# PEER V experts 0 to 119 with standing weights and moving tokens; fetched V rows scaled on ScalarE and summed on Pool

## What is computed

```python
def step(args):
    xc, ic, gc = args
    u = expert_u[ic]
    hval = jnp.einsum('cd,chkd->chk', xc, u).astype(jnp.float32)
    a = (gc * jax.nn.gelu(hval, approximate=False)).astype(xc.dtype)
    return jnp.einsum('chk,chkd->cd', a, expert_v[ic])
...
h = h + peer_ffn(rms_norm_2(h, norm_ffn_g[l]), ...)
return rms_norm_2(h, norm_final_g)
```

## Time and profile before

| | before |
|---|---|
| median of 3 runs | 1364.8 us (1364.66 to 1365.86) |
| the profiled execution | 1366.88 us |
| its span, first to last instruction | 1365.1 us |
| TensorE busy | 1349.6 us, 99% |
| VectorE busy | 1060.6 us, 78% |
| ScalarE busy | 818.7 us, 60% |
| Pool busy | 161.5 us, 12% |
| DMA, mean over the span | 202 GB/s |

### The profile page before, as it was taken

The page is one execution under the profiler, slowest core; times in us unless marked ns, Lnnn a source line. Parts: engine busy times, 40 slices in busy tenths (PEclk is TensorE's granted clock), DMA queues, the critical chain, the costliest instruction groups (busy, mean ns, idle before and its releaser), DMA issues.

```text
span 1365.1 us, 21297 instructions
## 1 busy us (share of the span) xinstructions
PE 1349.6 (99%) x7896; PEld 1169.7 (86%) x7896; DVE 1060.6 (78%) x1965; ACT 818.7 (60%) x1568; POOL 161.5 (12%) x128
## 2 busy tenths in 40 slices
PE   8999999999999999999999999999999999999998
PEld 6998888888898888789999999999877777777776
DVE  6878676666787567679999899998887777777775
ACT  6876555555665554555556988886554444544444
POOL 3002030000000000000001100001333332333200
PEclk9999999999999999999999999999999999999999
DMA  6533466566544446655655544445889877777763
GB/s 223 185 120 116 136 221 187 189 194 189 167 159 137 141 139 228 203 169 172 214 188 189 193 157 153 157 156 184 298 285 348 291 286 267 280 291 287 274 197 100
DMA packets 77372, 275.38 MB, mean 202 GB/s; under 512 B 9845, under 2 KB 10357, under 8 KB 76886
## 3 DMA queue, kind: packets, MB, share of 16 engines
q1 hardware_dynamic: 67462, 239.52, 53.0%
q0 software_dynamic: 9808, 34.51, 6.6%
HBM read 270.94 MB, written 2.10 MB: 200 GB/s over the span
## 4 chain that ended last, share of the span: by engine, by line
PE 91%; DVE 4%; ACT 2%; issue 1%; DMA 1%; POOL 0%; SPq 0%; POOLq 0%; ACTq 0%; DVEq 0%
PE bank L2335 89%; DVE wl L624 1%; PE bank L2433 1%; DMA raw<-in_wts 1%; PE bank L2421 1%; ACT wh L1688 1%; DVE rows L1562 0%; ACT kdz L1694 0%; DVE St L814 0%; DVE x L1123 0%; DVE sgt L1121 0%; DVE t L774 0%; DVE us L1553 0%; DVE sg L768 0%; DVE St L811 0%
## 5 line engine op out<-in xcount | busy, mean ns | idle before, releaser
L624 DVE TENSOR_TENSOR wl<-raw,wh 128x1024 fp32r<-128x1024 f32 x429 | 523.0, 1226 | 178.3 <-ACT wh L1688 174.0
L1688 ACT ACTIVATE wh<-raw 128x1024 fp32r<-128x1024 f32 x429 | 449.1, 1055 | 240.8 <-PE bank L2335 232.4
L2335 PE MATMUL bank<-hTb,wh 128*128 128x224 f32 (+4 forms) x2208 | 560.8, 332 | 1.8 <-DVE wl L624 1.8
L2335 PE MATMUL bank<-wh,hTb 128*128 128x512 f32 (+1 forms) x1496 | 431.1, 395 | 2.2 <-DVE hTb L658 1.5
L2335 PE MATMUL bank<-hTb,wl 128*128 128x224 f32 (+2 forms) x1640 | 426.7, 274 | 0.0
L2335 PEld LDWEIGHTS bank<-hTb,wh 128*128 128x128 f32 (+1 forms) x2208 | 372.2, 190 | 26.7 <-ACT ga L2217 1.8
L2335 PEld LDWEIGHTS bank<-wh,hTb 128*128 128x128 f32 (+1 forms) x1496 | 267.5, 180 | 78.3 <-DVE hTb L1605 2.5
L2335 PEld LDWEIGHTS bank<-hTb,wl 128*128 128x128 f32 (+1 forms) x1640 | 312.1, 190 | 6.1
L2335 PE MATMUL bank<-wl,hTb 128*128 128x512 f32 (+1 forms) x748 | 247.6, 392 | 0.0
L2335 PEld LDWEIGHTS bank<-wl,hTb 128*128 128x128 f32 (+1 forms) x748 | 134.4, 180 | 36.2
L601 POOL DMA_INDIRECT rows<-in_u_rows,expert x32 | 55.9, 1745 | 299.0 <-DVE dots L1562 295.3
(11 more groups left out here) (410 smaller groups left out, 1382.9 us busy)
## 6 DMA issues: line engine op xcount, KB each, us to landing
raw<-in_wts SPq DMA_DIRECT2D x441, 512.0 KB, 3.5
x<-in_x SPq DMA_DIRECT2D x4, 256.0 KB, 7.4
sk<-in_sk SPq DMA_DIRECT2D x1, 1024.0 KB, 7.1
spill<-x SPq DMA_DIRECT2D x1, 1024.0 KB, 7.4
x<-spill SPq DMA_DIRECT2D x1, 1024.0 KB, 6.4
gb<-in_g_ffn SPq DMA_DIRECT2D x1, 512.0 KB
gb<-in_norm_mix_g SPq DMA_DIRECT2D x1, 512.0 KB
gb<-in_norm_ffn_g SPq DMA_DIRECT2D x1, 512.0 KB, 4.2
```

What stands on the lines that cost most here:

```text
L624: e.tensor_tensor(b[:, :], raw[u % RAW][:, :], a[:, :].bitcast(F), ALU.subtract).then_inc(S("lo"), 1)
L1688: e.activation(parts_of(u)[0][:, :], raw[u % RAW][:, :], ACT.Copy).then_inc(S("hi"), 1)
L2335: return e.matmul(o, l, r, start=first, stop=last, skip_group_check=True)
```

## The change

**V units 0 to 119** (`DENSE` = 120) are computed like U units: `part_V` holds a slice of 128 output columns of V in the array, and moves 448 token columns with `wh` and 224 with `wl`. Slice k sums up in its own bank (`BANK_OF`), so that all eight banks are in use and hold the result transposed: 128 output columns by tokens. V units 120 to 127 stay as they were. Around the stage:

- U units 126 and 127 are finished inside the U loop. V units 0 and 1 first do the slices of banks 0, 1, 6, 7, and the others after the last U sum.
- V units 116 to 119 (`HOLD` = 4) are held together: first the slices in banks 0 to 3 for all four, then those in banks 4 to 7. ScalarE copies the low halves of the banks out (`lows_out`) and VectorE adds the others (`evacuated`), into places of `gates` that are no longer needed. After V unit 121 TensorE turns the eight sums back (16 transposes, into banks 4 to 7), and VectorE adds them into x (`add_turned`).
- The V rows: ScalarE multiplies the fetched row by its factor (`row_scaled`), in the row's own buffer, every 2.25 units from V unit 44 on; Pool adds it to `acc` (`added`). VectorE keeps the dots and the folding.
- `high_of` and `low_of` now stand ahead of `high` and `low` in each pass. The semaphore `one` is renamed `ready`.

```diff
+HOLD = 4
+DENSE = NE - 8
...
+        BANK_OF = (0, 1, 6, 7, 2, 3, 4, 5)
+        FIRST, SECOND = (0, 1, 4, 5), (2, 3, 6, 7)
...
+            def added(j):
+
+                e.wait_ge(S("ready"), 1 + j - SLOTS)
+                e.wait_ge(S("used"), used_by(j - 1))
+                e.tensor_tensor(acc[:, :], acc[:, :], rows[j % 3][:, :], ALU.add).then_inc(S("used"), 1)
+
             for j in range(2 * SLOTS):
+                if j >= SLOTS + 3:
+                    added(j - 2)
                 if j >= 3:
                     e.wait_ge(S("used"), used_by(j - 3))
...
+            for j in range(2 * SLOTS - 2, 2 * SLOTS):
+                added(j)
...
-                e.wait_ge(S("used"), used_by(j - 1))
-                e.scalar_tensor_tensor(out=acc[:, :], in0=t[:, :], scalar=factor[:, k:k + 1], in1=acc[:, :], op0=ALU.mult,
-                                       op1=ALU.add).then_inc(S("used"), 1)
...
+            def evacuated(ks, n):
+
+                for k in ks:
+                    e.wait_ge(S("u_out"), nth_sum("U", NE + n))
+                    e.tensor_tensor(sums_of(k), B[BANK_OF[k]][:, 0:TN], sums_of(k), ALU.add).then_inc(S("u_sum"), 1)
+                    n += 1
...
             for n in range(NE):
-                low(nth("D", "peer_expert_v_2", ORDER[n]) + LOOK)
                 if n + 2 < NE:
                     low_of(n + 2)
-                if n in (1, 2):
-                    summed(NE - 3 + n)
-                    gated(NE - 3 + n)
-                if n in at_v:
+                if n == DENSE - HOLD + 1:
+                    evacuated(FIRST, 0)
+                low(nth("D", "peer_expert_v_2", ORDER[n]) + LOOK)
+                if at_v.get(n, SLOTS + 1) <= SLOTS:
                     slot_taken(at_v[n])
-                elif n - 6 in (max(at_v), max(at_v) + 1, max(at_v) + 2):
-                    folded(n - 6 - max(at_v))
+                elif n in (DENSE - 3, DENSE - 2, DENSE - 1):
+                    folded(n - DENSE + 3)
+                if n == DENSE:
+                    evacuated(SECOND, 4)
+                elif n in (DENSE + 3, DENSE + 4):
+                    add_turned(n - DENSE - 3)
...
+                    e.activation(t[:, :], t[:, :], ACT.Copy, scale=factor[:, k:k + 1]).then_inc(S("ready"), 1)
+
+            rows_at = {after_dots + 3 + 9 * k // 4: SLOTS + k for k in range(SLOTS)}
...
+            def part_V(held, n, ks):
+
+                both = both_of(n)
+                for k in ks:
+                    c, b = two(128, k), B[BANK_OF[k]]
+                    mm(b[:, 0:2 * TN], held[0][:, c], both, n == 0, False)
+                    t = mm(b[:, 0:TN], held[1][:, c], both[:, 0, :], False, n == DENSE - 1)
+                return t
...
+            for n in range(2, DENSE - HOLD):
+                part_V(expert_of(n), n, range(8)).then_inc(S("done"), 1)
+            held = []
+            for n in range(DENSE - HOLD, DENSE):
+                held.append(expert_of(n))
+                t = part_V(held[-1], n, FIRST)
+            t.then_inc(S("half"), 1)
+            for n in range(DENSE - HOLD, DENSE):
+                part_V(held[n - DENSE + HOLD], n, SECOND).then_inc(S("done"), 1)
+            e.wait_ge(S("u_sum"), nth_sum("U", NE + 3))
```

More of the change, by code:

```diff
@@ L129, in program @@
         X0 = at[0]
-        ah = [sb(f"ah{i}", [128, 256], FR) for i in range(2)]
-        al = [sb(f"al{i}", [128, 256], FR) for i in range(2)]
+        ab = [sb(f"ab{i}", [128, 2, 256], FR) for i in range(2)]
+        ah, al = [t[:, 0, :] for t in ab], [t[:, 1, :] for t in ab]
         ge = [sb(f"ge{i}", [128, 256]) for i in range(2)]
@@ L659, in turn_low @@
                                 ALU.subtract).then_inc(S("hT_lo"), 1)
-            e.memset(one1[:, :], 1.0).then_inc(S("one"), 1)
+            e.memset(one1[:, :], 1.0).then_inc(S("ready"), 1)
             half_sums(0, 0)
@@ L1607, in vector @@
             at_u, at_v = slots_taken()
-            for n in range(GATED, NE - 2):
-                summed(n)
-                low(nth("U", ORDER[n]) + 2)
+            for n in range(GATED, NE):
+                if n < NE - 1:
+                    summed(n)
+                    low(nth("U", ORDER[n]) + 2)
+                else:
+                    low(nth("U", ORDER[n]) + 2)
+                    summed(n)
                 gated(n)
@@ L2313, in scalar @@
                     e.activation(factor[:, :], dots[:, :], ACT.Gelu).then_inc(S("used"), 1)
+                if n in rows_at:
+                    row_scaled(rows_at[n])
+                if n == DENSE:
+                    e.wait_ge(S("done"), nth("D", "peer_expert_v_2", ORDER[DENSE - 1]) + 1)
+                    lows_out(SECOND)
             half_squares(5, 0, sq6)
@@ L2439, in tensor @@
             e.wait_ge(S("in_ffn"), 16)
-            e.wait_ge(S("one"), 1)
+            e.wait_ge(S("ready"), 1)
             for n in range(2):
@@ new lines, in tensor @@
+            e.wait_ge(S("G"), NC)
+            held = []
+            for n in range(2):
+                held.append(expert_of(n))
+                part_V(held[n], n, (0, 1, 2, 3))
+            e.wait_ge(S("u_sum"), nth_sum("U", NE - 1))
+            for n in range(2):
+                part_V(held[n], n, (4, 5, 6, 7)).then_inc(S("done"), 1)
+            for n in range(2, DENSE - HOLD):
+                part_V(expert_of(n), n, range(8)).then_inc(S("done"), 1)
+            held = []
+            for n in range(DENSE - HOLD, DENSE):
+                held.append(expert_of(n))
+                t = part_V(held[-1], n, FIRST)
@@ new lines, in tensor @@
+            t.then_inc(S("half"), 1)
+            for n in range(DENSE - HOLD, DENSE):
+                part_V(held[n - DENSE + HOLD], n, SECOND).then_inc(S("done"), 1)
+            e.wait_ge(S("u_sum"), nth_sum("U", NE + 3))
+            for n in range(DENSE, NE - LAST):
+                e.wait_ge(S("al"), FFT + n + 1)
+                unit_D(("D", "peer_expert_v_2", ORDER[n]), *of_expert(n), 0, n == DENSE, False,
+                       tokens=(rows_of(0), rows_of(1)))
+                if n == DENSE + 1:
+                    e.wait_ge(S("u_sum"), nth_sum("U", NE + 7))
+                    for q in range(2):
+                        for k in range(8):
+                            p = e.transpose(B[4 + 2 * q + k // 4][0:rows_of(q), two(128, k % 4)],
+                                            sums_of(k)[:, 128 * q:128 * q + rows_of(q)], ident[:, :])
+                        p.then_inc(S("half"), 1)
```

60 lines of the change are left out of this document (38 added, 22 removed).

## The result

The changed kernel takes 1341.39 us (median of 4 runs, 1339.79 to 1341.67), the kernel before in the same series 1365.15 (4 runs, 1364.66 to 1365.86). The ratio is 0.9823, with a 95% interval of 0.9806 to 0.9840: 24 us faster. The profiled execution took 1339.79 us, with a span of 1337.9.

A forecast was written before the change was run, and what follows sets the result against it. TensorE, busy 99% of the span, was taken as the bound. The terms -29.4 - 1.4 + 2 + 1.3 + 2.0 + 1.8 = -23.7, say -24 us, gave a median of 1341 us (profiled 1342.9), range 1334 to 1353.

The forecast's parts named there:

- The unit: V units 0 to 119: each takes 2.515 us like a U unit, instead of 2.76; gain 29.4 us.
- The turn from U to V: Where U turns into V: the old loss of 1.4 us goes if VectorE is not behind; otherwise 0.
- The exclusion: V rows, units 44 to 113: VectorE and Pool exclude each other an instruction at a time; +2 us, between 0 and 10.
- A draw: V rows: over nine units VectorE plus Pool adds need 22.8 us against TensorE's 22.6, smoothed by four weight buffers.
- rival (a): V rows: the lock between VectorE and Pool binds, costing 10 us in place of 2; 1349 us, chance 0.2.
- The hold: Units 116 to 127: TensorE waits 1.3 us before unit 120 and 2.0 before the turnings, behind VectorE's folds and sums.
- The turnings: After V unit 121: sixteen transposes on TensorE at 0.10 to 0.11 us each; +1.8 us.
- (b): V rows: the fetching loop binds, from landings of about 8.6 us in every slot; slower than before, 1370 us, chance 0.05.
- (c): V units: not 2.515 us, as pairs change banks, or the change is worth half; 0.12 more each, 1355 us, chance 0.07.
- (d): Hold: VectorE is ahead, folds and sums coming earlier, and the lock costs nothing; 5 us better, 1336 us, chance 0.13.

The follow-up runs named there:

- rows_split_only: Kernel before with its old V units, but V rows scaled on ScalarE and summed on Pool, folds at units 117 to 119: 1364.32 us, ratio 1.0003.
- rows_on_vector: Changed kernel with the V rows put back on VectorE, Pool only fetching: 1340.14 us, ratio 0.9818.
- extra_pool_reads: Changed kernel with one more unused Pool product of 128 x 512 behind each of 29 later V row fetches: 1374.69 us, ratio 1.0070.
- rows_every_second: Changed kernel with ScalarE's scalings of V rows two units apart instead of 2.25: 1346.72 us.
- fetch_before_add: Changed kernel with each row's fetch issued on Pool ahead of the add of row j - 2, not behind it: 1339.59 us, ratio 0.9820.

## Why the prediction was right

The forecast was 1341 us; 1341.4 was measured. The mechanism was right in the terms that carry it: the unit, the two waits of the hold and the turnings add up to -24.3 us in the forecast and to -30.0 + 1.9 + 2.3 + 1.7 = -24.1 by the profile. That the sum came to -24 as well has some luck in it, since its two other terms, -1.4 for the turn and +2 for the exclusion, nearly cancel and neither is shown. Term by term, from the profile of the change:

- **The unit, -29.4**: 2.510 us instead of 2.515, so -30.0 by 120 x (2.76 - 2.510). Changing banks costs nothing, and the excess of about 17 ns per matmul carried over from the U stage. The Trainium skill (TensorE: Matmul & The Clock Gate, Back-to-back issue gap) gives its formula for an isolated matmul; this stream does not follow it, and the estimate of 37 us made from it would have been 7 us off. This was the step that decided everything, and rows_split_only and rows_on_vector show that the gain is there without the split and not with the split alone.
- **The turn from U to V, -1.4**: not shown. In the profile of the change no gap lies in units 0 to 19. But rows_split_only keeps the old turn and has no gap there either: from the first matmul of its V stage to the last it took 353.8 us, where the kernel before took 355.0. What the prediction read as the price of the old turn was for the most part one wait of TensorE for the token low part, ahead of 1019.09 us, that one profile of the old turn has and the other has not. Against rows_split_only the V stage of the change is 24.4 us shorter, as the other terms add up.
- **The exclusion, +2**: the mechanism was right to the instruction. An add takes 2.39 us at the least (I took 2.45 from twice the product of 512) and holds VectorE for 2.2. Its cost is not one number: next to nothing in one profile, 3.1 us in the other, and nothing in four profiles of later versions. For the medians the other terms already make -24.1, or -25.5 with the turn, and -24 was measured, so 0 to 1.5 us are left for the exclusion; the 2 us are not contradicted and not shown. "A draw" was the right word, and extra_pool_reads and rows_every_second show how near the edge it is: at a spacing of 2 units 7 us are lost, with ScalarE's waits for rows in it, and rival (a), 1349, would have been nearly there.
- **The hold, +1.3 and +2.0**: 1.92 and 2.28. Right in place and cause, 0.6 and 0.3 too small. The low part of unit 120 started 0.2 us later than I had it, the two folds took 1304.87 - 1302.29 = 2.58 from start to start where I had 2.35 (they do not overlap their neighbours as VectorE's other operations do), and TensorE began 0.1 after the token low part's end.
- **The turnings, +1.8**: 1.72.
- **The rivals**: (b) is out by the result and by fetch_before_add, but its limit was wrong: by its own terms, 2 x 5.66 - 1.06 - 1.14 - 2.55, it decides from a landing of 6.6 us and not of 8.6. V rows landed after 6.1 us in the median in the change (5.7 before), and ScalarE's waits of 3.0 and 9.9 us for them show how close that was. (c) is out by the 2.510 us. (d) was half right: the exclusion cost next to nothing in one execution, but VectorE was not ahead at the hold.
- **Not in the sum**: the V stage began at 1002.25 instead of 1003.88. This is a wait of TensorE for a low part late in the U stage, which was 1.8 us in the profile before and 0.5 and 0.6 in this one. In rows_split_only, whose U stage and V units are the old ones, it began at 1001.47. So it comes and goes between executions, and is no gain of the change. With it the profiled executions differ by 27.1 us and the medians by 24: had the sum been judged against the profiled forecast of 1342.9 alone, it would have seemed 3 us off.

The half of the change on which the prediction spends the most words, the split, is worth nothing: VectorE was not the bound before and is not the bound after. With the rows on VectorE it has 2.25 x 1.44 + 1.28 = 4.5 of 5.65 us per slot; with them on Pool, 2.25 x 1.44 + 2.2 = 5.4. Moving an operation off VectorE cost it more of its time than keeping it.

## What to carry to other kernels

When TensorE is 99% busy, take the duration of a new form of matmul from a stage of the same kernel that already runs it, from start to start over many, and not from columns over clock. Before work moves from VectorE to Pool, compare what it takes on VectorE with what it takes on Pool, since a Pool instruction that reads SBUF stops VectorE's two-input instructions for nearly its whole length (2.2 us of 2.4 here); Pool is free only for what just writes or fetches. Where a stage empties many accumulators in a row, put nothing in the emptying engine's order between the sums and the operand that the next matmul waits for.

## What was not expected of the hardware

- The fetch instruction of a V row took 0.95 us in the median on Pool in the changed kernel, and 1.94 with the fetch ahead of the add (it was 1.97 with the rows on VectorE). Line L622 of the change, then L620 of fetch_before_add (min/median/max ns):

```profile
L622 POOL DMA_INDIRECT rows<-in_v_rows,expert x32: 944/951/1979, 1097.2 to 1281.2; - x32
```

```profile
L620 POOL DMA_INDIRECT rows<-in_v_rows,expert x32: 936/1938/1984, 1096.5 to 1275.4; - x32
```

  Why a fetch right behind an add is twice as quick is open; in rows_split_only, where it also follows an add, it took 1.38 to 1.86 us. It never delayed VectorE.
- TensorE's granted clock fell behind the hold's waits in some executions (0.80 and 0.63 in rows_on_vector, behind both; 0.62 from 1304 to 1308 us in fetch_before_add, behind the first alone) and not in others with the same waits (1.00 in the change's profile).
- In the first third of the V stage DMA ran at a share of 0.96 and 361 GB/s, weights landed up to 10 us after their issue, and ScalarE waited 30 us for them in all (none in the kernel before, from 1010 to 1110 us). TensorE lost 0.3 us by it, at 1055.18, so the four weight buffers hid nearly everything. The prediction had costed this at 0 from 300 GB/s at 0.81, and was nearer to a bound there than it said.
